# Fused two-block layer, one core: the second block's two attentions by pairs of heads between the projections, stick-breaking by sigmoids and a product scan

## What is computed

```python
F = cumsum(log_sigmoid(fa + b_forget))
# forgetting attention ("fox"), 8 heads, s <= t
o_fox = softmax(qa_t . ka_s / 8 + F[t] - F[s]) @ va
# stick-breaking attention ("sb"), 8 heads, s < t
beta = sigmoid(qb_t . kb_s / 8)
A[t, s] = beta[t, s] * prod over s < j < t of (1 - beta[t, j])
o_sb = A @ vb
merged = sigmoid(ga) * (o_fox @ w_fox) + sigmoid(gb) * (o_sb @ w_sb)
x = x + gate1 * (merged @ w_out)
```

## Time and profile before

| | us |
|---|---|
| median of 3 runs (1778.73 to 1781.58) | 1781.45 |
| the profiled execution | 1777.71 |
| its span | 1775.9 |
| PE busy | 1624.5 (91%) |
| DVE busy | 841.8 (47%) |
| ACT busy | 789.1 (44%) |
| POOL busy | 638.7 (36%) |

### The profile page before, as it was taken

The page is one execution under the profiler, slowest core; times in us unless marked ns, Lnnn a source line. Parts: engine busy times, 40 slices in busy tenths (PEclk is TensorE's granted clock), DMA queues, the critical chain, the costliest instruction groups (busy, mean ns, idle before and its releaser), DMA issues.

```text
span 1775.9 us, 19626 instructions
## 1 busy us (share of the span) xinstructions
PE 1624.5 (91%) x7391; PEld 1245.6 (70%) x7391; DVE 841.8 (47%) x1439; ACT 789.1 (44%) x1222; POOL 638.7 (36%) x397
## 2 busy tenths in 40 slices
PE   7988899999999999999979999879999689999993
PEld 6664566888777877777848677557887377777772
DVE  5248884242236354543351330110002579999994
ACT  5216784222343132323334453672223357777772
POOL 3335574445655444454524214114546010000003
PEclk9998999999999999999979999889999889999996
DMA  6410002222236575765213122002226279999954
GB/s 239 145 58 12 1 1 90 95 83 95 95 107 237 201 248 191 240 227 174 84 48 98 45 95 89 18 1 71 95 95 241 83 280 391 392 392 395 392 210 167
DMA packets 78972, 276.23 MB, mean 156 GB/s; under 512 B 9556, under 2 KB 11140, under 8 KB 78872
## 3 DMA queue, kind: packets, MB, share of 16 engines
q1 hardware_dynamic: 69984, 246.00, 39.0%
q10 hardware_dynamic: 6584, 20.52, 3.1%
q0 software_dynamic: 2304, 8.39, 1.3%
HBM read 244.43 MB, written 30.45 MB: 155 GB/s over the span
## 4 chain that ended last, share of the span: by engine, by line
PE 67%; DVE 12%; ACT 8%; issue 4%; DMA 4%; POOL 4%; SPq 1%; another core or an unknown queue 0%; PEldq 0%; ACTq 0%; DVEq 0%; POOLq 0%
PE ps L415 14%; PE ps L419 14%; PE ps L416 14%; PE ps L907 3%; DMA RAW<-in_w_ff 3%; PE ps L903 2%; PE ps L904 2%; DVE RS L293 2%; DVE TMP L1424 2%; PE ps L921 2%; PE ps L922 2%; PE ps L925 2%; PE ps L784 1%; POOL RS L293 1%; PE ps L673 1%
## 5 line engine op out<-in xcount | busy, mean ns | idle before, releaser
L293 POOL TENSOR_TENSOR RS<-RAW,RS 128x1024 fp32r<-128x1024 f32 x174 | 423.6, 2436 | 521.8 <-ACT RS L288 521.8
L288 ACT ACTIVATE RS<-RAW 128x1024 fp32r<-128x1024 f32 x306 | 318.9, 1057 | 278.3 <-DMA RAW<-in_w_ff 115.4
L415 PE MATMUL ps<-RH,RS 128*128 128x512 f32 x928 | 374.8, 404 | 34.1 <-POOL RH L2189 13.3
L419 PE MATMUL ps<-RH,RS 128*128 128x512 f32 x928 | 367.6, 396 | 0.9 <-POOL RS L293 0.9
L416 PE MATMUL ps<-RH,RS 128*128 128x512 f32 x928 | 368.4, 397 | 0.0
L415 PEld LDWEIGHTS ps<-RH,RS 128*128 128x128 f32 x928 | 178.0, 192 | 84.5 <-POOL RH L2189 15.7
L419 PEld LDWEIGHTS ps<-RH,RS 128*128 128x128 f32 x928 | 178.3, 192 | 41.0 <-POOL RS L293 1.8
L416 PEld LDWEIGHTS ps<-RH,RS 128*128 128x128 f32 x928 | 178.4, 192 | 37.9 <-issue 1.7
L419 PE MATMUL ps<-RA,RS 128*128 128x512 f32 x416 | 165.8, 399 | 0.0
L416 PE MATMUL ps<-RA,RS 128*128 128x512 f32 x416 | 164.1, 394 | 0.0
L415 PE MATMUL ps<-RA,RS 128*128 128x512 f32 x416 | 164.1, 394 | 0.0
(11 more groups left out here) (340 smaller groups left out, 2509.8 us busy)
## 6 DMA issues: line engine op xcount, KB each, us to landing
RAW<-in_w_ff SPq DMA_DIRECT2D x64, 512.0 KB, 4.4
RAW<-in_w_gate SPq DMA_DIRECT2D x46, 512.0 KB, 6.5
RAW<-in_w_up SPq DMA_DIRECT2D x45, 512.0 KB, 7.1
RAW<-in_w_down SPq DMA_DIRECT2D x39, 512.0 KB, 7.5
PB<-in_ada SPq DMA_DIRECT2D x24, 512.0 KB, 3.8
TB<-in_ada SPq DMA_DIRECT2D x24, 512.0 KB, 3.5
xs<-TB SPq DMA_DIRECT2D x23, 512.0 KB, 6.7
M<-in_w_down SPq DMA_DIRECT2D x17, 512.0 KB, 5.9
```

The source lines that it names most:

```text
L288: act.activation(RS[:, spl[n], 0, :], raws[slot[n]], ACT.Copy).then_inc(*HI.up(n))
L293: eng.tensor_tensor(RS[:, s, 1, :], raws[slot[n]], hif(RS[:, s, 0, :]), ALU.subtract).then_inc(*mark.up(n))
L415: pe.matmul(b[:, :], wh, xh, start=(k == 0), stop=False)
L419: last = pe.matmul(b[:, :], wl, xh, start=False, stop=(k == K - 1))
```

## The change

The second block's attentions are done in eight steps of two heads, pairs 0 to 3 fox, pairs 4 to 7 stick-breaking, and each step's parts stand between projection tiles in every engine's order. The forget tile comes first, the first three ga tiles come before the last pairs. Of each list below only the core is shown, "..." marks what is left out.

The weight plan and the buffers:

```diff
-    for name in ("w2_qa", "w2_fa", "w2_ka", "w2_va", "w2_qb", "w2_kb", "w2_vb"):
-        whole(name)
+    for name, us in (("w2_fa", (0,)), ("w2_qa", (0, 1, 2, 3)), ("w2_ka", (0, 1, 2, 3)), ("w2_qb", (0,)),
+                     ("w2_va", (0, 1, 2, 3)), ("w2_qb", (1, 2, 3)), ("w2_kb", (0, 1, 2, 3)), ("w2_ga", (0,)),
+                     ("w2_vb", (0, 1, 2, 3)), ("w2_ga", (1, 2))):
+        plan.extend((name, u, "split") for u in us)
     for m in range(0, 8, 2):
-        plan += [("w2_ga", m, "split"), ("w2_ga", m + 1, "split"), ("w2_fox", m // 2, "split")]
+        plan += [("w2_ga", u, "split") for u in (m, m + 1) if u > 2] + [("w2_fox", m // 2, "split")]
         plan += [("w2_gb", m, "split"), ("w2_gb", m + 1, "split"), ("w2_sb", m // 2, "split")]
...
-    QA = KB = PC
+    QP = PC
+    KP = [M[:, k, :] for k in range(4)] + [RAW2[:, 2 + k // 2, 512 * (k % 2):512 * (k % 2) + 512] for k in range(4)]
     VA = [VV[:, 0, :], VV[:, 1, :], TAB[:, 0, :], TAB[:, 1, :]]
-    FB = [TMP[:, 0, :], TMP[:, 1, :]]
-    ABT = TMP[:, :, :].rearrange("p a n -> p (a n)")[:, 0:1280]
+    IB = [[M[:, 3, 384:512], M[:, 2, 256:512], M[:, 3, 0:384], M[:, 7, :]],
+          [M[:, 1, 384:512], M[:, 2, 0:256], M[:, 1, 0:384], M[:, 0, :]]]
```

PE. `pair_scores` makes both heads' scores (64 rows each) and adds the mask; `pair_turn` transposes; `pair_values` multiplies by the values into bank 7. All other banks are one ring of seven (`RB`), of which a pair's scores take six and a pair's turn six:

```diff
+        def pair_scores(n):
+            p = n % 4
+            pe.wait_ge(*A(("ev", ("w2_qa" if n < 4 else "w2_qb", p))))
+            pe.wait_ge(*A(("ev", ("w2_ka" if n < 4 else "w2_kb", p))))
+            for i in (3, 2, 0, 1):
+                x, o = NBK[i]
+                w = 128 * (i + 1)
+                bs = [ps["pk", n, a, x] if o else take(("pk", n, a, x), RB) for a in range(2)]
+                for a in range(2):
+                    h = slice(64 * a, 64 * a + 64)
+                    pe.matmul(bs[a][:, o:o + w], QP[h, p, 128 * i:128 * i + 128], KP[n][h, 0:w], start=True, stop=False,
+                              skip_group_check=True)
+                for a in range(2):
+                    last = pe.matmul(bs[a][:, o + w - 128:o + w], identb[:, :], (maskb if n < 4 else maskt)[:, :],
+                                     start=False, stop=True, skip_group_check=True)
+                    if i != 2:
+                        last.then_inc(*P.up(("psc", n, a, x)))
+
+        def pair_turn(n):
+            for a in range(2):
+                if n < 4:
+                    pe.wait_ge(*A(("ppt", n, a)))
+                pe.wait_ge(*G(("ppt", n, a)))
+                for j in (0, 1, 3, 2):
+                    x, o = TPX[j]
+                    b = ps["ptp", n, a, x] if o else take(("ptp", n, a, x), RB)
+                    for ii in range(j, 4):
+                        c = OFP[ii] + 128 * j
+                        last = pe.transpose(b[:, o + 128 * (ii - j):o + 128 * (ii - j) + 128],
+                                            PN[n % 2][a][:, c:c + 128], identf[:, :])
+                    if j != 1:
+                        last.then_inc(*P.up(("ptp", n, a, x)))
+
+        def pair_values(n):
+            b = take(("po", n), (7,))
+            pe.wait_ge(*V(("ev", ("w2_va" if n < 4 else "w2_vb", 3))))
+            for j in range(4):
+                x, _ = TPX[j]
+                for a in range(2):
+                    if j < 3:
+                        pe.wait_ge(*freed(("ptp", n, a, x)))
+                    h = 128 * (n % 4) + 64 * a
+                    last = pe.matmul(b[64 * a:64 * a + 64, 128 * j:512], VA[j][:, h:h + 64],
+                                     TB[:, a, PACK[j]:PACK[j] + 512 - 128 * j], start=(j == 0), stop=(j == 3),
+                                     skip_group_check=True)
+            last.then_inc(*P.up(("ppv", n), ("po", n)))
+
...
+        def projected(name, *us):
+            for u in us:
+                dense(name, u, RH, 0, 8, None, RB)
+
+        dense("w2_fa", 0, RH, 0, 8, lambda k: V(("h2", k)), RB)
+        projected("w2_qa", 0, 1, 2, 3)
+        projected("w2_ka", 0, 1)
+        pair_scores(0)
+        projected("w2_ka", 2)
+        pair_scores(1)
+        projected("w2_ka", 3)
+        pair_turn(0)
+        pair_scores(2)
+        projected("w2_qb", 0)
+        dense_rows("w2_va", RH, RB)
+        pair_values(0)
+        pair_turn(1)
+        pair_scores(3)
+        projected("w2_qb", 1)
+        pair_values(1)
+        pair_turn(2)
+        projected("w2_qb", 2)
+        pair_values(2)
+        pair_turn(3)
+        projected("w2_qb", 3)
+        pair_values(3)
+        projected("w2_kb", 0, 1)
+        pair_scores(4)
+        projected("w2_kb", 2)
+        pair_scores(5)
+        projected("w2_kb", 3)
+        pair_turn(4)
+        pair_scores(6)
+        projected("w2_ga", 0)
+        dense_rows("w2_vb", RH, RB)
+        pair_values(4)
+        pair_turn(5)
+        pair_scores(7)
+        projected("w2_ga", 1)
+        pair_values(5)
+        pair_turn(6)
+        projected("w2_ga", 2)
+        pair_values(6)
+        pair_turn(7)
+
+
```

ACT, for stick-breaking: two sigmoids for each bank part, sigmoid(z) to SBUF and sigmoid(-z) in place in PSUM. For fox the exponential stays as it was; the block of 512 columns is scaled by ACT, the other three by POOL, and ACT evicts the narrow transposes, DVE the others:

```diff
+        def pair_weights(n):
+
+            if n >= 4:
+                for x, o, w in SEGS:
+                    for a in range(2):
+                        b = ps["pk", n, a, x][:, 0:w]
+                        act.wait_ge(*P(("ptp", n - 2, a, 2)))
+                        act.wait_ge(*P(("psc", n, a, x)))
+                        act.activation(PN[n % 2][a][:, o:o + w], b, ACT.Sigmoid).then_inc(*A.up(("psg", n, a, x)))
+                        act.activation(b, b, ACT.Sigmoid, scale=-1.0).then_inc(*A.up(("pex", n, a, x)))
+                return
```

DVE: a product scan from the last key to the first gives what is left of the stick; POOL multiplies it with sigmoid(z), shifted by one key:

```diff
+        def pair_left(n):
+
+            for i in (3, 2, 0, 1):
+                x, o = NBK[i]
+                w = 128 * (i + 1)
+                for a in range(2):
+                    if n > 4:
+                        dve.wait_ge(*G(("pbr", n - 1, a, i)))
+                    dve.wait_ge(*A(("pex", n, a, x)))
+                    dve.tensor_tensor_scan(IB[a][i][:, ::-1], ps["pk", n, a, x][:, o:o + w][:, ::-1],
+                                           small[:, 2:3].broadcast_to([128, w]), 1.0, ALU.mult, ALU.add).then_inc(
+                        *V.up(("plf", n, a, i), ("ev", ("pk", n, a, x))))
+
...
+        def pair_scale(n):
+
+            for a in range(2):
+                pool.wait_ge(*V(("prc", n, a)))
+                for i in (2, 0, 1):
+                    pd = PN[n % 2][a][:, OFP[i]:OFP[i] + 128 * (i + 1)]
+                    pool.tensor_scalar(pd, pd, stat[:, 2, 2 * (n % 2) + a, i:i + 1], None, ALU.mult).then_inc(
+                        *G.up(("ppt", n, a)))
+
+        def pair_break(n):
+
+            for i in (3, 2, 0, 1):
+                o, w = OFP[i], 128 * (i + 1)
+                for a in range(2):
+                    pool.wait_ge(*A(("psg", n, a, NBK[i][0])))
+                    pool.wait_ge(*V(("plf", n, a, i)))
+                    pd = PN[n % 2][a][:, o:o + w - 1]
+                    tt(pd, pd, IB[a][i][:, 1:w], ALU.mult, ("pbr", n, a, i), ("ppt", n, a))
+
```

For fox DVE's `pair_shift` is the instruction of line 1628 in the new order, `pair_inverse` the reciprocal of line 1633, and `pair_outs` copies four banks of transposes to TB. POOL's order of work (`tiles_of` is the low halves; ACT and DVE follow the same order of steps):

```diff
+        tiles_of("w2_fa", (0,))
+        tiles_of("w2_qa", range(4))
+        tiles_of("w2_ka", (0, 1, 2))
+        pair_scale(0)
+        tiles_of("w2_ka", (3,))
+        pair_scale(1)
+        tiles_of("w2_qb", (0,))
+        pair_scale(2)
+        tiles_of("w2_va", range(4))
+        tiles_of("w2_qb", (1,))
+        pair_scale(3)
+        tiles_of("w2_qb", (2, 3))
+        tiles_of("w2_kb", (0, 1, 2))
+        pair_break(4)
+        tiles_of("w2_kb", (3,))
+        pair_break(5)
+        tiles_of("w2_ga", (0,))
+        pair_break(6)
+        tiles_of("w2_vb", range(4))
+        tiles_of("w2_ga", (1,))
+        pair_break(7)
+        tiles_of("w2_ga", (2,))
```

SP stores F itself (before, ACT did) and waits for the scan there; it reads two rows of F a pair:

```diff
+        def forget_rows(n):
+            for a in range(2):
+                f = 2 * (n % 2) + a
+                if n >= 2:
+                    sp.wait_ge(*V(("pmx", n - 2, a, 1)))
+                sp.dma_start(TMP[:, f, :], t["nf"][2 * n + a:2 * n + a + 1, :].broadcast_to([128, 512])).then_inc(
+                    *LD[f"fb{f}"].up(n))
+
...
+            elif plan[n][:2] == ("w2_qa", 1):
+                sp.wait_ge(*V("fscan"))
+                sp.dma_start(t["nf"], TMP[0:8, 3, :]).then_inc(*LD["nf"].up(0))
+            elif plan[n][:2] == ("w2_qa", 3):
+                sp.wait_ge(*LD["nf"](0))
+                forget_rows(0)
+                forget_rows(1)
+            elif plan[n][:2] == ("w2_ka", 3):
+                forget_rows(2)
+            elif plan[n][:2] == ("w2_qb", 0):
+                forget_rows(3)
```

More of the change, by code:

```diff
@@ L434, in dense_rows @@
                     for i in range(4):
-                        b = take((name, i), (banks[i],)) if k == 0 else ps[name, i]
+                        b = take((name, i), banks) if k == 0 else ps[name, i]
                         xh, xl = (R[:, x, k, 128 * i:128 * i + 128] for x in (0, 1))
@@ L571, in tensor @@
         fin(QKV[14])
[L574 to L607, removed]
-                if 1 <= n <= N:
-                    m = n - 1
-                    for j in (0, 1, 3, 2):
-                        bi, o = TPL[j]
-                        if o == 0:
```

(58 more changed lines are left out.)

446 lines of the change are left out of this document (177 added, 269 removed).

## The result

The kernel after takes **1703.68 us** (median of 4 runs, 1697.25 to 1708.04), the one before 1780.09 beside it (4 runs, 1774.97 to 1781.58): ratio 0.9573, 95% interval 0.9536 to 0.961. The forecast was 1704.0, the range 1690 to 1730. Run again later beside nine runs of before, the same kernel took 1703.3 us, ratio 0.9575 [0.9555, 0.9595].

The account below looks back on a forecast made before the run. PE was taken to bound the kernel, with 143.3 us of attention stretches without projections; pairs 66.7 + first values 1.6 + waits 1.5 = 69.8 us stay exposed, 73.5 less, so 1777.7 - 73.5 = 1704.2, forecast 1704, range 1690 to 1730.

Parts of the forecast that it names:

- The three stretches without projections: Second block's attention before: fox 47.5, first stick-breaking scores 3.0, stick-breaking 92.9, together 143.3 us, worth their cost in the span.
- Scores 3.7 us: PE's scores of a pair: 2.44 us, eight masks 0.44, and 0.2 four times for changing form; bounds 2.88 to 4.24.
- Values and turn: PE's other work per pair of heads: values 2.31 us, turn 2.33, as in the first block.
- First values: PE waits while DVE copies va and vb before the first values: 0.78 us, twice, 1.6 in the sum.
- After the turns: Scores 2, 3, 6, 7 directly follow a turn that filled six banks; 1.5 us for these waits together.
- The chain of stick-breaking: Scores 4 to turn 4: sigmoids, scans 6.1 us, products 6.4; done after about 10 us, covered by some 5 us.
- POOL's queue: Products and fox scales stand before low halves of later weight tiles; 6 us or more left, cost nothing.
- fox's softmax: Shift, exponent, inverse, scale in pairs 0 to 3: each turn comes 11 us or more after its scores, cost nothing.
- SP's loads: SP waits for the forget scan with ka tile loads behind it; covered by 4.6 us, cost nothing.
- (a): Rival: backward scans from PSUM take double, DVE needs 12 us a pair, +14 us, 1718; chance 0.14 for 1712 to 1732.
- (c): Rival: slower than before, 1780 and more, if a 512-column scan takes 5 to 6 us; chance 0.03, unseen waits included.
- (d): Rival: waits and form changes cost nothing, gain 83.1 us, 1694.6; chance 0.05 for below 1695.

Follow-up runs that it names:

- the last version: Kernel after with masks behind scores, start only on a bank's first score, `pair_done(4)` earlier, first values waiting per quarter of v: 1695.55 us, 0.9535 of before.

## Why the prediction was right

**What bounded the kernel.** The three stretches without projections were worth their length in the span. The run without interleaving and the run without suffix matmuls show both halves of that: PE stood behind waits, and its own matmul count in stick-breaking was not what set the length.

**Scores 3.7 us.** Measured 3.71. The change of form cost 0.31 there and back instead of 0.2, but three times, not four, as the last masks stand before a 128-row tile: 0.92 for the 0.8 of the sum; the scores alone were 0.08 cheaper than the row. The Trainium skill (TensorEngine Tiling (Array Packing), Tiling Modes) says that such a change drains the engine and gives no size. The runs agree that a change costs time, and add the size: without any drain I had 2.88 us for the group, it took 3.71, and with the masks in one row 2.79.

**Values and turn.** 2.31 and 2.33, as the first block's.

**Waits.** First values 0.8 us twice: predicted 1.6, measured 1.7. After the turns 1.5 predicted, none measured: DVE's four copies start with the first bank, and PE fills the rest of the turn meanwhile. That term of the sum was 1.5 us too large. It alone would have made the stage 1.5 shorter than forecast; it was 0.1 longer. What the sum lacked are the joins between projection and group. Two places of PE's timeline, out of a group and into one:

```profile
1074.59 0.48 PE L415 MATMUL ps<-RH,RS 128*128 128x512 f32 x1
1074.90 0.40 PE L416 MATMUL ps<-RH,RS 128*128 128x512 f32 x1
1075.13 0.39 PE L419 MATMUL ps<-RH,RS 128*128 128x512 f32 x1
...
1079.90 0.39 PE L419 MATMUL ps<-RH,RS 128*128 128x512 f32 x1
1080.21 0.70 PE L712 MATMUL ps<-RAW,PC 64*128 64x512 f32 x2
```

The step is 0.31 us at each side instead of 0.23, so 0.16 for each time PE leaves the projections. It does that 13 times in the stage after and three times before: 10 more by 0.16 is 1.6 us, an estimate from these two joins. So two errors of 1.5 us cancelled. That the median, 1703.68, came out at the forecast 1704 to 0.3 us is luck: I took the stage's gain from the profiled execution, 1777.7; taken from the median before, 1780.09, the 73.5 us give 1706.6.

**The chain of stick-breaking.** Scan 1.21, as the SBUF row. POOL's eight products take 5.8 us, not 6.4 to 7. In pair 4 they end at 1082.1, 11.2 us after its scores began at 1070.87 where I had 10; a table load of ACT (1.28 us) is in that and wasn't in my count. The turn starts at 1089.47: 7.4 us of cover where I gave 5. By my own numbers it should have been 8, since I held 10 us from the start of scores 4 against 14.6 from their end. The thin place is another one. Turn 4 needs the banks of pair 5, whose scans run from 1082.94 for 5.82 us to 1088.76, 0.7 us before the turn starts. The doubled scans used that up: it waited 1.5 us.

**POOL's queue, fox's softmax, SP's loads.** Nothing, as claimed: no wait names them. The forget scan took longer than the row I had (last section), and the 4.6 us of cover held.

**Rivals.** (a) did not happen, and the doubled scans priced it: 19.3 us in the stage against 14, with the waits in other places and the clock on top. I had not followed bank 7 through DVE's order, so I missed that `pair_done(4)` is queued behind the scans of pair 7. (c), slower, needed a scan of 5 us. (d), 1694.6 without waits and form changes, is about what the last version comes to, 1695.55, with one form change a pair and the joins left.

## What to carry to other kernels

Count what PE stands beside, not what PE does: eighty matmuls beside a chain of ACT were free, and without them PE stood longer and the matmuls behind the stops ran at a lower granted clock. When attention goes between projections, give each chain the time of one or two tiles, follow every bank through the order of the engine that gives it back, and double one engine's work at a time to find the thin place. Keep matmuls of another height together: eight masks in one row cost 0.43 us, spread over the group 0.9 more.

## What the runs showed of the hardware

**Two SBUF inputs and POOL.** The forget scan (8x512) took 1.21 us before and 3.03 after, and 3.03 to 3.05 in each variant of after. DVE's line and POOL's:

```profile
943.41 3.03 DVE L1887 TENSOR_TENSOR_SCAN TMP<-TMP 8x512 f32<-8x512 f32 x1
```

```profile
942.97 5.67 POOL L292 TENSOR_TENSOR RS<-RAW,RS 128x1024 fp32r<-128x1024 f32 x2 [5.53 <-ACT RS L287]
```

The first of two low halves had begun 0.4 us before the scan. At its 2.4 us it ends near 945.4, the scan 1.1 later, at 946.44, and the second half 2.2 after that, at 948.64: one after the other. The run with scans from SBUF shows the same from both sides. The Trainium skill (SBUF — State Buffer, section SBUF: two separate sides) says that a DVE operation with two SBUF inputs and a GpSimd operation that reads SBUF exclude each other for the whole instruction, whichever starts first; the trace agrees (2.67 against 1.20, 1.86 against 1.09, and 1.22 for scans of PSUM). Reading the new scans from PSUM is thus part of why they cost 1.21 beside POOL.

**A start flag reaches over the bank.** The two kernels with masks last differ in the start flag of the second block of a bank alone, and their outputs differ. The Trainium skill (PSUM — Partial Sum Buffer, The four PSUM rules) says that the flag clears the written state of the whole bank in the quadrants it touches, so that a mask that comes later replaces the first block's scores; the outputs agree with that, and no time shows it.

**The granted clock after a stop.** 0.52 in the 6 us after a wait of 3.6 us; 4.46 us for values of 2.31 after one of 6.9, and 4.0 to 4.6 us for eight scores of 2.40 in the kernel without suffix matmuls. Behind the wait of 1.8 us, with masks last, the values took 2.30 us (1123.90 to 1126.20), so nothing was lost there beside the wait.
